# RMSNorm column sums: squares as TensorE weights, and a reduction on VectorE, in a two-block fp32 model kernel

## The reference, cut to what matters

```python
def rmsnorm(x, g, eps=NORM_EPS):
    x32 = x.astype(jnp.float32)
    y = x32 * lax.rsqrt(jnp.mean(x32 * x32, axis=-1, keepdims=True) + eps)
    return (y * g.astype(jnp.float32)).astype(x.dtype)
```

## Time and profile before

| | us |
|---|---|
| median of 3 runs | 4074.2 |
| lowest and highest | 4072.64, 4080.19 |
| the profiled execution | 4072.64 |
| its span | 4070.8 |
| PE matmul busy | 3571.1 (88%) |
| DVE busy | 1769.9 (43%) |
| ACT busy | 1353.5 (33%) |
| POOL busy | 1330.7 (33%) |
| mean granted TensorE clock | 0.927 |

### The profile page before, as it was taken

How to read it: one execution, slowest core, us unless ns; L and a number is a source line. 1 busy time by engine, 2 the same in 40 slices (tenths; PEclk the granted TensorE clock), 3 DMA queues, 4 the chain that set the end, 5 groups by cost and what they waited for, 6 DMA issues and landing times.

```text
span 4070.8 us, 50977 instructions
## 1 busy us (share of the span) xinstructions
PE 3571.1 (88%) x17608; PEld 2869.6 (70%) x17608; DVE 1769.9 (43%) x3100; ACT 1353.5 (33%) x2246; POOL 1330.7 (33%) x683
## 2 busy tenths in 40 slices
PE   6898998888998999888799997889899997769998
PEld 5677876677777777666578875778788886546666
DVE  1534244434235332565432223556666556444443
ACT  3322233322232222444332233433333433324443
POOL 4344432344434444222134431333333333100001
PEclk8899999999998999999899998899999998879999
DMA  4322221223222322111122321011011011100001
GB/s 157 108 99 98 98 73 62 83 98 119 88 88 103 114 88 93 57 52 57 31 80 96 98 86 47 27 36 37 32 40 36 31 36 35 54 16 21 21 21 37
DMA packets 72966, 269.77 MB, mean 66 GB/s; under 512 B 8096, under 2 KB 8096, under 8 KB 72096
## 3 DMA queue, kind: packets, MB, share of 16 engines
q1 hardware_dynamic: 64944, 236.14, 17.4%
q10 hardware_dynamic: 7920, 32.25, 2.2%
HBM read 264.16 MB, written 4.19 MB: 66 GB/s over the span
## 4 chain that ended last, share of the span: by engine, by line
issue 47%; PE 27%; POOL 17%; DVE 5%; ACT 2%; POOLq 1%; ACTq 0%; DVEq 0%
POOL wl L392 16%; PE ps L469 12%; PE ps L903 2%; PE ps L885 2%; PE ps L482 1%; PE ps L912 1%; PE ps L484 1%; PE ps L483 1%; PE ps L772 1%; PE ps L785 1%; PE ps L822 1%; POOL xs L417 1%; DVE rstd L1789 1%; PE ps L886 1%; POOL xe L422 1%
## 5 line engine op out<-in xcount | busy, mean ns | idle before, releaser
L392 POOL TENSOR_TENSOR wl<-raw,wh 128x1024 fp32r<-128x1024 f32 x438 | 1140.9, 2605 | 2609.6 <-ACT wh L1079 2609.6
L1079 ACT ACTIVATE wh<-raw 128x1024 fp32r<-128x1024 f32 x438 | 463.0, 1057 | 1190.0 <-PE ps L469 510.3
L469 PE MATMUL ps<-hh,wh 128*128 128x512 f32 (+1 forms) x1856 | 756.0, 407 | 30.0 <-DVE hl L1568 28.4
L469 PE MATMUL ps<-hl,wh 128*128 128x512 f32 (+1 forms) x1856 | 738.1, 398 | 0.0
L469 PE MATMUL ps<-hh,wl 128*128 128x512 f32 (+1 forms) x1856 | 736.7, 397 | 0.0
L469 PEld LDWEIGHTS ps<-hh,wh 128*128 128x128 f32 x1856 | 367.5, 198 | 134.9 <-issue 40.5
L469 PEld LDWEIGHTS ps<-hh,wl 128*128 128x128 f32 x1856 | 365.9, 197 | 78.5
L469 PEld LDWEIGHTS ps<-hl,wh 128*128 128x128 f32 x1856 | 368.2, 198 | 72.3 <-issue 1.7
L482 PE MATMUL ps<-fh,wh 128*128 128x512 f32 x768 | 311.5, 406 | 5.6 <-DVE fl L1612 3.0
L483 PE MATMUL ps<-fl,wh 128*128 128x512 f32 x768 | 305.1, 397 | 0.0
L484 PE MATMUL ps<-fh,wl 128*128 128x512 f32 x768 | 304.4, 396 | 0.0
(11 more groups left out here) (311 smaller groups left out, 5530.0 us busy)
## 6 DMA issues: line engine op xcount, KB each, us to landing
raw<-stream_dram SPq DMA_DIRECT2D x438, 512.0 KB, 3.3
modw<-mod_dram ACTq DMA_DIRECT2D x48, 512.0 KB, 3.7
x<-xT_dram SPq DMA_DIRECT2D x1, 2048.0 KB, 8.5
side<-ctxT_dram ACTq DMA_DIRECT2D x2, 1024.0 KB, 7.4
park_dram<-x ACTq DMA_DIRECT2D x1, 2048.0 KB, 6.3
x<-park_dram ACTq DMA_DIRECT2D x1, 2048.0 KB, 7.9
out_dram<-x SPq DMA_DIRECT2D x8, 256.0 KB, 2.2
side<-memT_dram SPq DMA_DIRECT2D x1, 1024.0 KB, 4.8
```

Source lines behind the costliest of these rows:

```text
L392: nc.gpsimd.tensor_tensor(wl[:, u % RING, :], raw[:, u % RAW, :], wh[:, u % RING, :].bitcast(FP32), ALU.subtract).then_inc(s_lo, 1)
L469: last = nc.tensor.matmul(bank, a[:, s, w], b[:, k, c0:c1], start=(k == 0 and a is wh and b is hi), stop=(k == KD - 1 and a is wl))
L1079: nc.scalar.activation(wh[:, u % RING, :], raw[:, u % RAW, :], ACT.Copy).then_inc(s_hi, 1)
```

## The change

The operands of the sum are swapped: the squares become the weights, and one column of ones moves. A sum for 128 tokens then is one column on 128 partitions; blocks no longer accumulate in the bank but go to columns of their own (`KD*c + k`), 32 in all. A new reduction on DVE adds the eight columns of each group of tokens into `rstd[:, 8:12]`, with a new semaphore `ss_ready`; ACT takes the root of 128x4 elements after it, DVE the reciprocal of 128x4. The spread takes a column of the reciprocals, repeated, as weights, and the identity moves. A memset of `rt` goes.

```diff
@@ norm_sum (PE)
             for c in range(width // P):
-                last = nc.tensor.matmul(B[7][32 * c:32 * c + 32, 0:P], ones[:, 0:32], sqr[:, k % 2, chunk(c)],
-                                        start=(k == 0), stop=(k == KD - 1))
+                last = nc.tensor.matmul(B[7][:, KD * c + k:KD * c + k + 1], sqr[:, k % 2, chunk(c)], ones[:, 0:1],
+                                        start=True, stop=True)
@@ norm_spread (PE)
-                last = nc.tensor.matmul(B[6][:, chunk(c)], ident[:, 32 * c:32 * c + 1].to_broadcast([P, P]), rstd[:, 0:P],
-                                        start=True, stop=True)
+                last = nc.tensor.matmul(B[6][:, chunk(c)], rstd[:, c:c + 1].to_broadcast([P, P]), ident, start=True, stop=True)
@@ root (ACT)
-            act.wait_ge(sq_used, 8 * n + 8)
-            rows = slice(0, width // P * 32)
-            nc.scalar.activation(rt[rows, 0:P], B[7][rows, 0:P], ACT.Sqrt, bias=eps6[rows, 0:1],
+            act.wait_ge(ss_ready, n + 1)
+            nc.scalar.activation(rt[:, 0:width // P], rstd[:, KD:KD + width // P], ACT.Sqrt, bias=eps6[:, 0:1],
                                  scale=1.0 / D).then_inc(rt_ready, 1)
@@ DVE
+        def sums(name, width):
+
+            dve.wait_ge(sq_used, 8 * NORM[name] + 8)
+            nc.vector.tensor_reduce(rstd[:, KD:KD + width // P], B[7][:, 0:width // P * KD].rearrange("p (c k) -> p c k", k=KD),
+                                    AX.X, ALU.add).then_inc(ss_ready, 1)
+
         def reciprocal_root(name, width):
+            sums(name, width)
             dve.wait_ge(rt_ready, NORM[name] + 1)
-            nc.vector.reciprocal(rstd[:, 0:P], rt[:, 0:P]).then_inc(rs_ready, 1)
+            nc.vector.reciprocal(rstd[:, 0:width // P], rt[:, 0:width // P]).then_inc(rs_ready, 1)
             dve.wait_ge(rb_ready, NORM[name] + 1)
@@
-        nc.vector.memset(rt[:, 0:P], 1.0)
```

More of the change, by code:

```diff
@@ L281, in build @@
     sq_ready, sq_used, rt_ready = sem("sq_ready"), sem("sq_used"), sem("rt_ready")
-    rs_ready, rb_ready = sem("rs_ready"), sem("rb_ready")
+    ss_ready, rs_ready, rb_ready = sem("ss_ready"), sem("rs_ready"), sem("rb_ready")
     tmp_ready, h_hi, h_ready = sem("tmp_ready"), sem("h_hi"), sem("h_ready")
```

## The result

| | before | after |
|---|---|---|
| median, us | 4074.85 (4 runs) | 4106.76 (4 runs) |
| lowest and highest | 4072.64, 4080.19 | 4105.76, 4114.51 |
| ratio, 95% interval | | 1.0080 (1.0065 to 1.0094) |
| span of the profiled execution | 4070.8 | 4107.7 |
| PE matmul busy | 3571.1 | 3644.1 |

The kernel is 32 us (0.8%) slower. That is the time of the first rival (4107), not of the predicted case (4088).

What follows compares the result with a forecast made beforehand. TensorE, busy in 88% of the span, was taken as the bound. Terms 13.7 - 5.8 + 4.5 + 1.4 + 0.6 - 0.2 = +14.2 us on 4072.64 gave 4086.8, as a median 4088; range 4077 to 4107.

Steps and rivals of the forecast that it cites:

- first rival: Clock stays at the lower level in runs of one-column matmuls, in sums standing alone and tails: +33 us, 4107, chance 0.25.
- predicted case: The main forecast for the whole kernel: +14.2 us, median 4088, spanning 4080 to 4096 alone, chance 0.50.
- Step 4: Sums standing alone in ffn0 and lat0: +4.5 us with a clock rise after 24 of 64 records, up to +14.5.
- Step 3: Tails of six norms: -0.97 us each, -0.5 of it from a faster spread; -5.8 in all, bounds -2.8 and -8.8.
- Step 5: Sums standing alone in mem and ctx0, 32 records each: +0.3 to +1.9 us, taken +0.7 each, +1.4 in all.
- step 6: Norm last, 64 fast records: +1.1 us, less up to 1.0, taken +0.6; lat1 -0.2; ctx1, short and warm, 0.
- Steps 1 and 2: Sums between large matmuls: 16 singles at +0.34 us, +5.4; pairs +4.1 in four norms, +4.2 in ffn1 and ffn3; +13.7.
- Reduction, root, reciprocal: Small operations after the sums in a tail, with hand-overs: 0.20 + 0.27 + 0.19 + 0.20 = 0.86 us until the spread.
- lat1: Norm where DVE side blocks cover the slower sums; reduction and root come after them, 0.81 against 0.95 + 0.05 us: -0.2.
- The clock falls in the stream: Rival: each of ten pairs of sums between large matmuls lowers the clock, losing 1.7 us each: 17 more, 4105, chance 0.08.
- Swallowed: Rival: other waits in the down projections shorten by what the sums grow: +0.5 us, 4075, the same, chance 0.12.
- Weight loads follow each other faster: Rival: loads overlap the matmuls, records starting 0.025 us apart, so sums shorten: -15 us, 4059, chance 0.05.

Runs made afterwards that it cites:

- hybrid: Sums as before; a DVE copy and one selecting matmul put tokens on partitions, then the changed kernel's small root, reciprocal and spread: 4068.85 us, ratio 0.9985 to before.
- stream_only: New form only in the six norms ending a stream of projections (pool, ffn1, ffn2, diff, ffn3, final), other seven as before: 4082.87 us, ratio 1.0022 to before.
- cols128: Changed kernel with 128 columns of ones moving instead of one, same weight loads, blocks accumulating, reduction kept: 4086.79 us, ratio 1.0028 to before.
- tiled: Changed kernel with squares loaded 32 tokens at a time into four column groups, four times as many records: 4068.76 us, ratio 0.9990 to before.
- accum: Changed kernel with the one-column sums accumulating in PSUM and no DVE reduction, the root reading the sums directly: 4101.94 us, ratio 1.0069 to before.
- cols128_root: cols128 without the DVE reduction, the root reading one of 128 equal columns from PSUM: 4083.96 us, ratio 1.0026 to before.

## Why the prediction was wrong, point by point

*Step 4 failed*, in the sentence "I take a rise after 24 of the 64 records, my choice between ctx0's early one and none". There was no rise: 64 records at 0.215 us took 13.79, as the bound of the same step had it (13.8), and ffn0 and lat0 cost 7.0 and 7.5 (bounds 7.0 and 7.5, taken 2.0 and 2.5). In ctx0 before, the clock came up under matmuls that move 128 columns; I carried that row over to one of another form. And the row itself was thin. The rise stood only in the last quarter of those sums, and in hybrid and stream_only, which keep the old sums in ctx0, it does not come:

```profile
2455.80:2459.20 3.40, 3.09 (x24) 1.37 (x24) 0.44 (x1) 2.05 (x6) 0.00 (x0) 0.50 0.91 386
2459.30:2460.30 1.00, 0.83 (x10) 0.29 (x8) 0.00 (x0) 0.53 (x2) 0.00 (x0) 1.00 0.59 246
...
2446.60:2451.30 4.70, 4.26 (x32) 1.70 (x32) 0.40 (x1) 2.64 (x7) 0.00 (x0) 0.50 0.79 335
2466.10:2470.80 4.70, 4.26 (x32) 1.70 (x32) 0.41 (x1) 2.65 (x7) 0.00 (x0) 0.50 0.79 335
```

(Before in two parts, then hybrid and stream_only.) So the same sums met either clock, and the row was no ground for a rise in ffn0 and lat0. cols128 shows what the choice was worth: its 4086.8 is what the kernel takes where the clock does come up, and my case was 4088. That these two are so near is partly luck: laid beside before, its ffn0 and lat0 cost 4.7 us together (4.5 taken) and its tails -6.9 (-5.8), but its stream cost 9.6 where I had 13.7.

The same choice stood in other terms. *Step 3* gave half of a faster spread to each tail; the spread stayed at 2.07, and in ffn1 and ffn3 the clock fell while the tail's sums ran, so that the step from last square to spread grew by 0.7 where -0.47 was forecast (pool and final -0.42, ffn2 and diff about 0, as the clock fell half way through their last sums). *Step 5* was 2.1 us short and *step 6* 4.4 for last, where the clock fell part way (0.63), and 1.2 for ctx1, which I had called warm.

*Steps 1 and 2*: the size of a sum was right, their number wrong, in the description of the kernel too. `FF_TAIL` puts block 5 after the last unit, and `MIX_TAIL` the third pair, where PE waits for the last squares anyway; so 12 singles, 4 pairs and 4 pairs lie in the stream: 4.1 + 4.1 + 2.8 = 11.0. Measured 9.8: in the four norms after a down projection the units' other waits took back about 0.3 each. The third pair in out_memory delays the last squares instead, by 0.2.

*Reduction, root, reciprocal*: 0.82 for 0.86, right. *lat1*: -0.2, right.

*The rivals*: the clock staying down had 0.25 and 4107, and the measured 4106.8 is its time; its terms for ffn0, lat0, mem, ctx0 and last, 14.5 + 3.8 + 4 = 22.3 together, came to 7.0 + 7.5 + 3.5 + 5.0 = 23.0. The rest of the agreement is luck: its stream was 3.9 us too dear (13.7 for 9.8) and its tails 3.9 too cheap (-2.8 for +1.1). "The clock falls in the stream" did not happen where it was placed: a window over the stream of ffn1 shows 1.00.

```profile
750.00:763.00 13.00, 13.00 (x72) 11.07 (x70) 2.28 (x4) 3.14 (x4) 3.25 (x2) 1.00 0.25 82
```

"Swallowed" was small: 1.2 us in all. Weight loads follow each other faster only in tiled, narrow and in separate column groups; full-width ones kept 0.11 us from start to start. What was missing in the prediction was weight: the nearest form said nothing for a rise, and the choice had no row of its own.

What stays open: what the clock does with a number of moving columns between 1 and 128, which wasn't tried; and how much of the shifts in the stages between the norms belongs to a kernel, for each trace is one execution.

## What to carry to other kernels

Swapping operands so that fewer columns move does not make a matmul cheap: in fp32 the full-width weight load then is the price (0.11 us a record warm, 0.21 cold), and narrow loads in separate column groups were a way to pay less. A long run of one-column matmuls stayed at the lower clock from end to end here, so cost such a run at that level unless a row of that very form shows the higher one, and in more than one execution. And when small steps stand behind a table load, make them fit its shadow (tiled, hybrid): that gave the gain that the change was losing elsewhere.

## What the runs showed of the hardware

- 64 pairs of weight load and one-column matmul, PE shown busy 13.73 to 13.79 of 13.8 us or a little more: granted clock 0.50 throughout in both places of two kernels (after, accum). With 128 columns moving and the same loads: 0.74 to 0.84 on average over the same sums (cols128, cols128_root).
- 32 narrow records (32 weights wide, four column groups) take 0.43 us, as long as 8 old records with 128 moving columns; 8 full-width records with one column take 0.95, and with 128 columns 1.05.
- Groups in one PSUM bank can be summed column by column when only the first matmul of all has the start flag (accum, cols128). The Trainium skill (PSUM — Partial Sum Buffer, "The four PSUM rules", the point on hidden has_written bits) says that a matmul without the flag overwrites where the bit is clear; the sums of these two kernels come out as that says.
